# Moving four weight-row units of a modulation from the passes of a scan to three later norms

## What is computed

```python
mod = silu_c @ ada_w[layer] + ada_b[layer]
shift_m, scale_m, gate_m, shift_f, scale_f, gate_f = jnp.split(mod, 6, axis=-1)
...
h = modulate(rms_norm(x, norm_mix_w[layer]), shift_m, scale_m)
...
x = x + gate_m[:, None, :] * y
h = modulate(rms_norm(x, norm_ffn_w[layer]), shift_f, scale_f)
x = x + gate_f[:, None, :] * conv_ffn_2(h, ...)
```

## Time and profile before

| | |
|---|---|
| median of 3 runs | 1500.94 us (1498.19 to 1502.79) |
| the profiled execution | 1503.28 us |
| its span | 1501.3 us |
| TensorE matmul (PE) busy | 1451.2 us, 97% |
| TensorE weight load (PEld) busy | 1288.1 us, 86% |
| VectorE (DVE) busy | 1074.7 us, 72% |
| ScalarE (ACT) busy | 733.5 us, 49% |
| mean DMA rate | 183 GB/s |
| chain that ended last | PE 89%, DVE 6%, ACT 3% |

### The profile page before, as it was taken

How to read it: one execution, slowest core, us unless ns; L and a number is a source line. 1 busy time by engine, 2 the same in 40 slices (tenths; PEclk the granted TensorE clock), 3 DMA queues, 4 the chain that set the end, 5 groups by cost and what they waited for, 6 DMA issues and landing times.

```text
span 1501.3 us, 26563 instructions
## 1 busy us (share of the span) xinstructions
PE 1451.2 (97%) x10494; PEld 1288.1 (86%) x10494; DVE 1074.7 (72%) x1655; ACT 733.5 (49%) x969; POOL 6.8 (0%) x19
## 2 busy tenths in 40 slices
PE   7989999999999999999999999899999999999997
PEld 7886889999987889999887768679999899799996
DVE  6784878777856687777766755667777768677775
ACT  5553545444545554455465542645454533454442
POOL 0000000000000000000000000000000000000000
PEclk9999999999999999999999999999999999999999
DMA  7433745555456354554525665055545555555540
GB/s 308 155 140 119 278 161 187 196 182 195 175 209 269 119 191 169 193 194 173 194 109 225 233 247 209 29 198 197 195 171 195 195 196 172 193 197 177 187 168 29
DMA packets 39694, 275.02 MB, mean 183 GB/s; under 512 B 4528, under 2 KB 5680, under 8 KB 6960
## 3 DMA queue, kind: packets, MB, share of 16 engines
q1 hardware_dynamic: 38304, 265.82, 48.4%
q0 software_dynamic: 720, 6.82, 1.2%
q10 hardware_dynamic: 576, 1.05, 0.2%
HBM read 272.62 MB, written 1.05 MB: 182 GB/s over the span
## 4 chain that ended last, share of the span: by engine, by line
PE 89%; DVE 6%; ACT 3%; issue 1%; DMA 0%; DVEq 0%; ACTq 0%
PE L L1769 28%; PE D L1769 17%; PE L L1957 15%; PE L L1963 8%; PE N L1957 5%; PE N L1963 3%; PE M L1857 2%; PE N L1865 2%; PE D L1957 1%; DVE wlo L990 1%; PE D L1934 1%; PE D L2236 1%; DVE arena L1067 1%; PE D L1963 1%; PE D L1901 1%
## 5 line engine op out<-in xcount | busy, mean ns | idle before, releaser
L1769 PE MATMUL L<-h_all,whi 128*128 128x256 f32 (+1 forms) x1392 | 286.3, 305 | 15.8 <-DVE wlo L1279 6.9
L990 DVE TENSOR_TENSOR wlo<-raw,whi 128x2048 fp32r<-128x2048 f32 x106 | 242.3, 2287 | 67.2 <-ACT whi L497 67.1
L1957 PE MATMUL L<-h_all,whi 128*128 128x512 f32 x992 | 252.8, 396 | 4.4 <-DVE h_all L1039 3.2
L1769 PEld LDWEIGHTS L<-h_all,whi 128*128 128x128 f32 x1392 | 228.1, 197 | 32.8 <-issue 17.8
L497 ACT ACTIVATE whi<-raw 128x2048 fp32r<-128x2048 f32 x106 | 201.8, 1908 | 103.2 <-PE L L1769 87.0
L1152 DVE TENSOR_TENSOR wlo<-raw,whi 128x2048 fp32r<-128x2048 f32 x96 | 219.7, 2288 | 38.7 <-ACT whi L632 38.7
L1957 PEld LDWEIGHTS L<-h_all,whi 128*128 128x128 f32 x992 | 178.6, 190 | 41.6 <-DVE h_all L1039 5.4
L1769 PE MATMUL L<-h_all,wlo 128*128 128x256 f32 (+1 forms) x696 | 210.0, 302 | 0.0
L632 ACT ACTIVATE whi<-raw 128x2048 fp32r<-128x2048 f32 x96 | 183.0, 1906 | 0.0
L1769 PE MATMUL D<-hd_hi,whi 128*128 128x256 f32 x640 | 181.3, 283 | 0.0
L1769 PE MATMUL D<-hd_hi,wlo 128*128 128x256 f32 x640 | 181.1, 283 | 0.0
(11 more groups left out here) (306 smaller groups left out, 2243.2 us busy)
## 6 DMA issues: line engine op xcount, KB each, us to landing
raw<-in_units SPq DMA_DIRECT2D x250, 1024.0 KB, 4.8
arena<-in_band POOLq DMA_DIRECT2D x1, 2304.0 KB, 9.4
arena<-in_nax POOLq DMA_DIRECT2D x1, 1536.0 KB, 9.1
t<-in_mem ACTq DMA_DIRECT2D x4, 256.0 KB, 5.8
raw<-in_units SPq DMA_DIRECT2D x4, 256.0 KB, 5.4
x<-in_x SPq DMA_DIRECT2D x1, 1024.0 KB, 9.0
t<-in_ctx POOLq DMA_DIRECT2D x1, 1024.0 KB, 5.3
arena<-in_ctx POOLq DMA_DIRECT2D x1, 1024.0 KB, 7.2
```

The lines of the kernel that those rows point to most:

```text
L990: V.tensor_tensor(wlo[w][:], raw[v % RING][:], whi[w][:].bitcast(FP), ALU.subtract) \
L1769: ins = mm(dst, w[a], h[b], start=start and n == 0, stop=stop and n == 2, skip_group_check=True)
L1957: mm(bank[:], w[0][:, k, part * P:part * P + P], h_all[:, k, 0:512], start=k == 0, stop=False, skip_group_check=True)
```

## The change

The stream has other numbers of modulation units in its places: the scan's passes take 17 instead of 21, the norms ahead of ffn2, o_b and ffn3 four each. In the passes the middle unit of passes 1, 2, 4 and 6 goes. Because the groups of four shift, so do the places of the copies and turns; `turn(9)` comes in front of o_b's units, `turn(10)` behind o_b's first job, `turn(11)` inside ffn3's first chunk. VectorE's last `modulation` goes behind ffn3's first convolution. The weights are packed in the new order on the host.

```diff
-    ("e_hg0", 1, "fm", "lat"), ("e_hq1", 1, "fm", "lat"), ("ada_h0", 2, "ada", None),
-    ("e_fb1", 1, "fm2", "both"), ("ada_h1", 3, "ada", None), ("e_hi1", 1, "tm2", "both"), ("ada_h2", 3, "ada", None),
-    ("e_hg1", 1, "fm", "lat"), ("ada_h3", 1, "ada", None), ("e_nk0", 1, "fm2", "both"), ("ada_h4", 5, "ada", None),
+    ("e_hg0", 1, "fm", "lat"), ("e_hq1", 1, "fm", "lat"), ("ada_h0", 1, "ada", None),
+    ("e_fb1", 1, "fm2", "both"), ("ada_h1", 2, "ada", None), ("e_hi1", 1, "tm2", "both"), ("ada_h2", 3, "ada", None),
+    ("e_hg1", 1, "fm", "lat"), ("ada_h3", 1, "ada", None), ("e_nk0", 1, "fm2", "both"), ("ada_h4", 3, "ada", None),
...
-    ("e_out", 4, "fm", "mix"), ("ffn2", 2, "ffn", "lat"), ("ada_f2", 3, "ada", None), ("ffn2", 3 * NI - 2, "ffn", "lat"),
-    ("o_b", 2, "fm", "lat"), ("ada_o", 3, "ada", None), ("o_b", 2, "fm", "lat"),
+    ("e_out", 4, "fm", "mix"), ("ffn2", 2, "ffn", "lat"), ("ada_f2", 4, "ada", None), ("ffn2", 3 * NI - 2, "ffn", "lat"),
+    ("o_b", 2, "fm", "lat"), ("ada_o", 4, "ada", None), ("o_b", 2, "fm", "lat"),
...
-    ("ffn3", 2, "ffn", "lat"), ("ada_f3", 2, "ada", None), ("ffn3", 3 * NI - 2, "ffn", "lat"),
+    ("ffn3", 2, "ffn", "lat"), ("ada_f3", 4, "ada", None), ("ffn3", 3 * NI - 2, "ffn", "lat"),
...
-H_ADA = ADA["ada_h0"]
+H_ADA = [(), (0, None, 1), (2, None, 3), (4, 5, 6), (7, None, 8), (9, 10, 11), (12, None, 13), (14, 15, 16)]
+H_ADA = [[n if n is None else ADA["ada_h0"] + n for n in p] for p in H_ADA]
...
-                if 1 < e <= 2 * HGH:
+                if 1 < e <= 2 * HGH and H_ADA[e - 1][1] is not None:
                     rows_out()
...
             jobs("e_out", lambda n, j: square(x, n))
-            for _ in range(3):
+            for _ in range(4):
                 rows_out()
             root()
...
                 square(x, i)
-            for _ in range(3):
+            for _ in range(4):
                 rows_out()
             root()
...
             jobs("o_out", lambda n, j: square(x, n))
-            for _ in range(2):
+            for _ in range(4):
                 rows_out()
             root()
...
                 convolve(0)
+                if early:
+                    early()
                 upto(u0 + 3)
...
-                dve.wait_ge(R["ada_turned"], 10)
+                dve.wait_ge(R["ada_turned"], 9)
                 modulation(0, 16, 48, 2, [(2, 32, 0, "ffn_w2", 0)])
-                modulation(1, 0, 32, 3, [(3, 8, 0, "mix_w2", KB)])
+                modulation(1, 0, 24, 3, [(3, 8, 0, "mix_w2", KB)])
...
-                 {1: lambda: modulation(1, 32, 40, 4, [(4, 32, 0, "ffn_w2", KB)])})
+                 {1: lambda: modulation(1, 24, 40, 4, [(4, 32, 0, "ffn_w2", KB)])})
...
-            modulation(1, 40, 48, 5, [])
-            ffn("ffn3", 3, CENTRED3, lambda k: mod[:, 1, 40 + k, 0:1])
+            ffn("ffn3", 3, CENTRED3, lambda k: mod[:, 1, 40 + k, 0:1], early=lambda: modulation(1, 40, 48, 5, []))
...
-                    modulate(H_ADA + 3 * e - 3)
+                    modulate(H_ADA[e][0])
...
-                if e:
-                    modulate(H_ADA + 3 * e - 2)
+                if e and H_ADA[e][1] is not None:
+                    modulate(H_ADA[e][1])
                 job(H_BESIDE[e][-1])
...
-                    modulate(H_ADA + 3 * e - 1)
+                    modulate(H_ADA[e][2])
...
-            jobs("e_nv0", after={1: lambda: turn(9)})
+            jobs("e_nv0", after={1: lambda: turn(8)})
...
-            for n in range(3):
+            for n in range(4):
                 modulate(ADA["ada_f2"] + n, n == 0)
             ffn("ffn2", 2)
...
-            modulate(ADA["ada_o"])
-            modulate(ADA["ada_o"] + 1)
-            jobs("o_b", fresh=True, after={0: lambda: modulate(ADA["ada_o"] + 2)})
+            for n in range(4):
+                modulate(ADA["ada_o"] + n)
+            jobs("o_b", fresh=True, after={0: lambda: turn(10)})
...
             pe.wait_ge(R["mod_ready"], 4)
-            for n in range(2):
-                modulate(ADA["ada_f3"] + n)
-            turn(11)
-            ffn("ffn3", 3)
+            for n in range(4):
+                modulate(ADA["ada_f3"] + n, n == 0)
+            ffn("ffn3", 3, mid=lambda: turn(11))
```

More of the change, by code:

```diff
@@ L121 @@
 DENSE = [v for v in range(NU) if v not in ADA_UNITS]
-FILLS = {j.unit for n in ("ada_bd", "ada_o") for j in JOBS[n]}
+FILLS = {j.unit: len(JOBS[n]) for n in ("ada_bd", "ada_o") for j in JOBS[n]}
 def prior_job(v):
@@ L134, in ahead @@
 def ahead(v):
-    return v + 2 + (3 if v + 2 in FILLS else 0)
+    return v + 2 + FILLS.get(v + 2, 0)
 H_BESIDE = [JOBS["e_ff1"], JOBS["e_hg0"] + JOBS["e_hq1"], JOBS["e_fb1"], JOBS["e_hi1"],
             [JOBS["e_hg1"][0], JOBS["e_nk0"][0]], [JOBS["e_nk0"][1]], [JOBS["e_nk1"][0]], [JOBS["e_nk1"][1]]]
-H_ADA = ADA["ada_h0"]
+H_ADA = [(), (0, None, 1), (2, None, 3), (4, 5, 6), (7, None, 8), (9, 10, 11), (12, None, 13), (14, 15, 16)]
+H_ADA = [[n if n is None else ADA["ada_h0"] + n for n in p] for p in H_ADA]
 def pieces_beside(order, prefix):
@@ L1141, in residual, with ffn @@
                     rows(3)
-            def ffn(name, f, offsets, gate=None, scaled=True, g=None):
+            def ffn(name, f, offsets, gate=None, scaled=True, g=None, early=None):
                 u0 = JOBS[name][-1].unit - 3 * NI + 1
@@ L2337 @@
         ffn_units(up[1][:, FF:], up[1][:, :FF], a["ffn_w_down"][1]),
-        ev[4][:1], ev[5][:1], late[8:11], ev[3][:1], ev[6][:1], ev[4][1:], ev[7][:1], ev[3][1:], late[11:13],
-        ev[5][1:], late[13:16], ev[6][1:], late[16:19], ev[7][1:], late[19:20], ev[1][:1], late[20:25], ev[1][1:], late[25:32],
-        ev[0], ev[2], units(a["ev_w_out_2"][0]), f2[:2], late[32:35], f2[2:],
-        ob[:2], late[35:38], ob[2:], np.stack([oc, ou], 1).reshape(8, P, 2048), units(a["od_w_out_2"][0]),
-        f3[:2], late[38:], f3[2:],
+        ev[4][:1], ev[5][:1], late[8:11], ev[3][:1], ev[6][:1], ev[4][1:], ev[7][:1], ev[3][1:], late[11:12],
+        ev[5][1:], late[12:14], ev[6][1:], late[14:17], ev[7][1:], late[17:18], ev[1][:1], late[18:21], ev[1][1:], late[21:28],
+        ev[0], ev[2], units(a["ev_w_out_2"][0]), f2[:2], late[28:32], f2[2:],
+        ob[:2], late[32:36], ob[2:], np.stack([oc, ou], 1).reshape(8, P, 2048), units(a["od_w_out_2"][0]),
+        f3[:2], late[36:], f3[2:],
     ]
```

## The result

| | before | after |
|---|---|---|
| median | 1500.94 us (5 runs) | 1508.77 us (5 runs: 1506.37 to 1511.22) |
| ratio | | 1.0052, 95% interval 1.0039 to 1.0064 |
| span of the profiled execution | 1501.3 us | 1506.7 us |
| profiled execution | 1503.28 us | 1508.77 us |

The change makes the kernel 0.5% slower, 7.8 us by the medians; 1508.9 was forecast.

What follows compares the result with a forecast made beforehand. TensorE, busy 97% of the span, was taken as the bound. Terms -2.05 + 3.06 + 4.84 + 1.74 gave +7.6, with 0.4 for the clock +8.0: 1508.9 us against the median 1500.94, range 1503.5 to 1513.5.

Steps and rivals of the forecast that it cites:

- passes: Scan's passes: four units fewer -3.92, one turn fewer -0.43, a new wait in pass 5 +2.3; -2.05 us in all.
- norm ahead of ffn2: Ahead of ffn2: ScalarE's root waits for the fourth unit, its copy and the table load; +3.06 us.
- o_b (norm and first job): Ahead of o_b: root +5.39 later, then a unit less (-0.98) and turn 10 (+0.43) behind the first job; +4.84 us.
- norm ahead of ffn3: Ahead of ffn3: four units instead of two, root behind their copy, no table load; +1.74 us.
- clock, in ffn2's first chunk: A clock dip behind TensorE's longer idle time ahead of ffn2, mostly in the first chunk; +0.4 us, 0 to 1.7 a norm.
- stall in pass 5: Pass 5: ScalarE's copy call waits for pass 4's last unit ahead of the root, so TensorE waits 2.3 us at L2233.
- late load: o_b's norm: the fourth unit waits for its load, which uses the buffer of o_b's second unit; 2.1 us.
- turn inside the first chunk: ffn3's first chunk: turn 11 goes into the waits for blocks of h; uncovered it would be 0.43 us.
- (a): Late norms: the root does not wait for the copy, idle time swallows the units; sum -4.9, 1496.0 us; chance 0.08.
- (b): Norms and pass 5: table loads run ahead of copies, stall mostly hidden; +3.1 to +3.9, about 1504.5 us; chance 0.17.
- (c): Three norms: longer idle times each bring a half-clock stretch at full price; +12.7 in all, 1513.6 us; chance 0.08.
- (d): Two norms and pass 5: table loads on the path cost double, 5.2 us in all; 1514.1 us; chance 0.02.

Runs made afterwards that it cites:

- the version without the stall: Against the kernel after: in ScalarE's loop over the scan's rounds the third copy call stands behind the head's square root; 1502.24 us in one run.
- three_and_one: Against the kernel after: square root first in three norms and scan's rounds, o_b's fourth unit behind its first job, turn 10 behind the second; 1494.51 us, ratio 0.9953.
- the three versions: Against the kernel after: square root first in three norms and scan's rounds, with three arrangements of o_b's units, loads and copies; 1496.37, 1497.83 and 1494.51 us.
- f2_root_first: Against the kernel after: ahead of ffn2 alone, ScalarE takes the square root first and copies the rows behind h's second rounded block; 1506.52 us in one run.
- early_table: Against the kernel after: a one-column scrap square root ahead of ffn2 and o_b loads the table while ScalarE waits for the fourth unit; 1506.00 us in one run.
- o_stream: Against the kernel after: the four units ahead of o_b stand in the stream behind one o_b unit instead of two; 1506.39 us in one run.

## Why the prediction was right

Its time, 1508.9, is 0.1 us from the median. The mechanism was right in each of its places, but that closeness is luck: o_b's term was 1.3 us too small, and the passes (0.6), the clock (0.5) and ffn3 (0.1) together as much too large.

| term | forecast | stretch |
|---|---|---|
| passes | -2.05 | -2.64 |
| norm ahead of ffn2 | +3.06 | +3.05 |
| o_b (norm and first job) | +4.84 | +6.11 |
| norm ahead of ffn3 | +1.74 | +1.62 |
| clock, in ffn2's first chunk | +0.4 | -0.1 (ffn2) |
| sum | +8.0 | +8.0 |

**The passes.** The stall in pass 5 was 2.06 us against 2.3, with the mechanism as stated, save that 0.34 of it came already at the head turn (L2209), which waits for ScalarE's scaling. What the units gave was 4.9 us instead of 4.35 (the stretch of the version without the stall). From scores to scores, before against that version: pass 1 19.33 to 18.45, pass 2 19.07 to 17.26, pass 3 19.43 to 19.78, pass 4 19.04 to 17.51, pass 6 14.51 to 13.32. Pass 1, one unit less, gives 0.88; passes 2 and 4, a unit and a turn less, 1.81 and 1.53, against 1.4 by the rows. Pass 3, which has a turn more, takes 0.35 longer, and pass 6, a unit less alone, gives 1.18. Pass 2 shows where the forecast was short. From the start of L2236 to the first product with `wlo` in the job behind it there were 3.36 us before and 2.17 in the version with the root first, so that the unit between them was worth 1.19 and not 0.98; and the turn behind the outputs was worth 0.65 and not 0.43 (from L2253 to the unit behind it 1.11 us before, 0.46 without the turn). Both prices had been read at other neighbours, in pass 1. That no engine took over as the bound holds: VectorE's slack in pass 6 was enough.

**The norm ahead of ffn2** was right to 0.01 us, the load behind the copy included; two runs show it, one that takes the copy away (-3.05) and one that takes the load alone (-1.42, where 1.3 was the forecast's share).

**o_b.** The late load (2.41 us against 2.1), the copy and the table load behind it are all there. The term is 1.3 too small, 0.3 for the longer wait and the rest for want of the clock. TensorE waited 2.4 us, did one unit and waited 4 more, and by the two windows shown with the run that has o_b's units later, it ran at 1.2 GHz for (1 - 0.61) x 2 x 10.2 = 8.0 us up to 1201.2 and for (1 - 0.75) x 2 x 4.8 = 2.4 us behind it, 10.4 in all. The fourth unit so took 0.35 longer, and job 0's stretch is 8.58 where unit and turn exchanged would have made it 7.9. And the 8.43 of before is no clean base: it holds the stretch of the earlier trace rows, without which three_and_one has the same work done in 7.27. I put the clock's cost at the wrong norm: into ffn2's and not into o_b's, where the rows had a dip and the forecast two new waits beside it. There was a dip ahead of ffn2 too, in the window of its first chunk in the kernel after:

```profile
991.00:1001.00 10.00, 6.04 (x21) 3.79 (x18) 6.60 (x16) 7.23 (x12) 0.00 (x0) 0.83 0.93 392
```

It cost nothing: the chunk is fed slowly, and the ffn2 stretch is 0.1 us shorter than before.

**ffn3.** +1.62 against +1.74. The turn inside the first chunk is hidden (5.99 us against 6.02), and so is the late `modulation`.

**The rivals.** (a), the cover holds, fell as stated: the copy ended at 991.54, while the root was free 3.4 us behind the last sums' start (987.34 to 990.76 in the run with the root first), at 989.8. But it was the right picture of what the change could be: without the copies in the way -4.9 was its sum, and the medians of the three versions stand 3.5 to 6.9 us below before. (b) would have needed both the load ahead of the copy and a hidden stall, and neither came. (c) was right in that more half-clock time came, and wrong in the place and the price: about 1 us in o_b's norm and first job beyond what before pays there, nothing ahead of ffn2 and ffn3. (d), the double load, is ruled out by the run with the early table.

## What to carry to other kernels

A filler that ends with a hand-over on another engine is only as free as that engine's order lets it be: where the hand-over stands ahead of the step that ends the idle time, the filler lengthens it, one for one. Filling an idle time of 1.8 us with 0.9 us of work made it 4.0 us, and moving the hand-over behind that step gave it back. When units are regrouped, look at every place where "every fourth does more" now falls, on each engine, and at what its buffer's previous user is doing.

## What the runs showed that I had not expected

The granted clock is not the same in every execution of one kernel, nor of kernels that have the same waits: its mean over an execution lay between 0.986 and 0.991 in the five runs of the kernel after. Behind 0.34 + 1.71 us of waiting in pass 5 it fell in two of the four profiled executions with that stall (f2_root_first and early_table, but not the kernel after and o_stream), at a cost of 1.6 us each, and in the attention it fell in two of the last three versions. So a wait of this size costs its own time and, in some executions, 1.6 us more, and a single profile can be off by that. Behind the two waits of o_b's norm it fell for 10.4 us at once. To compare stretches between two fixed instructions, as here, was worth more than to compare spans.
